# Two rings for the split weights of a two-block mixer kernel: raw units and their low parts share six slots, high parts get five, and loads wait for TensorE

## The reference

```python
def first_block(x, ...):
    for layer in range(DEPTH):
        h = rms_norm(x, norm_mix_pre[layer])
        m = mixer_block(h, ...)                  # h @ w_in, three branches, gates, @ w_out
        x = x + rms_norm(m, norm_mix_post[layer])
        h = rms_norm(x, norm_ffn_pre[layer])
        x = x + rms_norm(swiglu(h, ...), norm_ffn_post[layer])
...
def second_block(x, c, ctx, ...):
    for l in range(DEPTH):                       # the context is updated in layer 0 alone
        hx = rmsnorm(x, norm1_w[l]) * (1.0 + sc1) + sh1
        mix_x, mix_c = token_mixers(hx, hc, ...) # h @ w_in, conv, mLSTM, attention, @ w_out
        x = x + g1 * mix_x
        hx = rmsnorm(x, norm2_w[l]) * (1.0 + sc2) + sh2
        x = x + g2 * conv_ffn(hx, ...)
```

## Time and profile before

| | |
|---|---|
| median of 3 runs | 2644.31 us (2641.03 to 2645.47) |
| the profiled execution | 2644.44 us, of it 2642.3 us span |
| granted TensorE clock | 0.999 on the mean |
| TensorE busy | 2603.2 us (99%) |
| TensorE loading weights | 2243.4 us (85%) |
| VectorE busy | 1487.3 us (56%) |
| ScalarE busy | 1340.1 us (51%) |
| GpSimd busy | 1666.2 us (63%) |
| HBM read | 382.53 MB, 145 GB/s over the span |

### The profile page before, as it was taken

One profiled execution on the slowest core, in us unless ns is written; L12 is line 12 of the kernel. 1 busy time (PEld: TensorE's weight loads), 2 busy tenths in 40 slices (PEclk: granted clock), 3 DMA queues, 4 the chain that ended last, 5 costly groups with the idle time before them and its releaser, 6 DMA issues.

```text
span 2642.3 us, 43046 instructions
## 1 busy us (share of the span) xinstructions
PE 2603.2 (99%) x15736; PEld 2243.4 (85%) x15736; DVE 1487.3 (56%) x2545; ACT 1340.1 (51%) x2671; POOL 1666.2 (63%) x1252
## 2 busy tenths in 40 slices
PE   8999999999999999999999999999999999999999
PEld 7998788899888887877788888888888889999888
DVE  6886533388654436855533333668654965235644
ACT  6475545556655553456343343442444575446655
POOL 6779788778887884422334345556554645558887
PEclk9999999999999999999999999999999999999999
DMA  6466676545867552221222223446542423335555
GB/s 220 133 188 209 209 241 190 167 133 160 255 211 223 182 179 91 88 65 56 65 71 80 72 88 114 133 144 225 204 135 85 142 84 109 105 118 161 169 181 162
DMA packets 216445, 386.24 MB, mean 146 GB/s; under 512 B 21952, under 2 KB 49856, under 8 KB 216256
## 3 DMA queue, kind: packets, MB, share of 16 engines
q1 hardware_dynamic: 216256, 383.66, 45.8%
HBM read 382.53 MB, written 1.05 MB: 145 GB/s over the span
## 4 chain that ended last, share of the span: by engine, by line
PE 44%; issue 33%; POOL 17%; DVE 4%; ACT 1%; DMA 0%; POOLq 0%; SPq 0%; DVEq 0%; ACTq 0%
POOL w_lo L1065 17%; PE bank L1130 12%; PE bank L1134 6%; PE bank L1114 6%; PE bank L1116 6%; PE bank L1115 6%; PE bank L1679 1%; PE bank L1230 1%; PE bank L1210 1%; PE bank L1211 1%; PE bank L1212 1%; PE bank L1652 1%; PE bank L1346 1%; DVE k_dec L2604 0%; DVE gdec L2599 0%
## 5 line engine op out<-in xcount | busy, mean ns | idle before, releaser
L1065 POOL TENSOR_TENSOR w_lo<-raw,w_hi 128x512 fp32r<-128x512 f32 x1248 | 1666.0, 1366 | 965.5 <-ACT w_hi L1733 964.4
L1733 ACT ACTIVATE w_hi<-raw 128x512 fp32r<-128x512 f32 x1248 | 719.0, 623 | 295.5 <-PE bank L1116 125.3
L1114 PE MATMUL bank<-hl,w_hi 128*128 128x256 f32 (+1 forms) x1920 | 659.8, 344 | 0.8 <-POOL w_lo L1065 0.3
L1116 PE MATMUL bank<-hl,w_lo 128*128 128x256 f32 (+1 forms) x1920 | 645.4, 336 | 0.0
L1115 PE MATMUL bank<-hl,w_hi 128*128 128x256 f32 (+1 forms) x1920 | 645.2, 336 | 0.0
L1114 PEld LDWEIGHTS bank<-hl,w_hi 128*128 128x128 f32 x1920 | 364.2, 190 | 44.1 <-issue 5.0
L1115 PEld LDWEIGHTS bank<-hl,w_hi 128*128 128x128 f32 x1920 | 364.4, 190 | 40.6 <-issue 3.6
L1116 PEld LDWEIGHTS bank<-hl,w_lo 128*128 128x128 f32 x1920 | 364.2, 190 | 38.0
L1130 PE MATMUL bank<-hl,w_hi 128*128 128x512 f32 x1296 | 361.4, 395 | 0.8 <-POOL w_lo L1065 0.5
L1130 PEld LDWEIGHTS bank<-hl,w_hi 128*128 128x128 f32 x1296 | 221.5, 188 | 31.8 <-issue 3.0
L1134 PEld LDWEIGHTS bank<-hl,w_lo 128*128 128x128 f32 x1296 | 197.7, 188 | 27.6
(11 more groups left out here) (353 smaller groups left out, 4225.3 us busy)
## 6 DMA issues: line engine op xcount, KB each, us to landing
raw<-stream SPq DMA_DIRECT2D x1248, 256.0 KB, 3.0
mix<-stream SPq DMA_DIRECT2D x64, 512.0 KB, 4.7
spare_lo<-stream SPq DMA_DIRECT2D x16, 512.0 KB, 5.0
spare_hi<-stream SPq DMA_DIRECT2D x16, 512.0 KB, 5.6
xs<-x_rows SPq DMA_DIRECT2D x4, 256.0 KB, 6.0
xs<-ctx_rows SPq DMA_DIRECT2D x1, 1024.0 KB, 6.5
out_rows<-xs SPq DMA_DIRECT2D x8, 128.0 KB, 2.9
dec<-decay SPq DMA_DIRECT2D x1, 768.0 KB, 6.7
```

The lines of the kernel that those rows point to most:

```text
L1065: nc.gpsimd.tensor_tensor(w_lo[:, unit % SPLIT, part], raw[:, unit % RAW, part], w_hi[:, unit % SPLIT, part], ALU.subtract).then_inc(lo_re ...
L1114: nc.tensor.matmul(acc, wh, x[:, 0, k, c0:c1], start=k == 0, stop=False)
L1116: last = nc.tensor.matmul(acc, wl, x[:, 0, k, c0:c1], start=False, stop=k == t.k - 1)
L1733: nc.scalar.activation(w_hi[:, n % SPLIT, part], raw[:, n % RAW, part], ACT.Copy).then_inc(hi_ready, 1)
```

## The change

The 44 KB of weight buffers per partition are cut anew. `raw` gets six slots instead of three. `w_lo` becomes a second name for the same bytes, so POOL writes the low part over the raw weights that it has just read. `w_hi` gets five slots instead of four. A load of unit n can then no longer follow POOL: it waits until TensorE has used unit n-6, once for both halves. ACT's copy of unit n waits for unit n-5 and stands one unit earlier in its program, wherever the place was counted with `SPLIT`. Weight loads have the key n-6 in SP's order. POOL's loop has 30 units in its body.

```diff
-RAW, SPLIT = 3, 4
+RAW, HIGH, FIRST = 6, 5, 3
...
-    order = [(n - RAW - SPLIT, 0, n) for n in range(N_UNITS)]
+    order = [(n - RAW, 0, n) for n in range(N_UNITS)]
...
+    at_raw = sbuf.at
     raw = sbuf.put("raw", [P, RAW, UNIT * P])
-    w_hi = sbuf.put("w_hi", [P, SPLIT, UNIT * P], F32R)
-    w_lo = sbuf.put("w_lo", [P, SPLIT, UNIT * P], F32R)
+    w_lo = nc.alloc_sbuf_tensor_at("w_lo", [P, RAW, UNIT * P], F32R, offset=at_raw)
+    w_hi = sbuf.put("w_hi", [P, HIGH, UNIT * P], F32R)
...
             def load(unit):
+                if unit >= RAW:
+                    kind, count = PLACE.free[unit - RAW]
+                    sp.wait_ge(tile_done if kind == "tile" else unit_used, count)
                 for j, part in enumerate(UNIT_HALVES):
-                    if unit >= RAW:
-                        sp.wait_ge(lo_ready, 2 * (unit - RAW) + j + 1)
                     sp.dma_start(raw[:, unit % RAW, part], stream[ADA_UNITS + unit][:, part])\
                         .then_inc(raw_loaded[unit % RAW][j], 16)
...
-            for unit in range(1, RAW):
+            for unit in range(1, FIRST):
...
-            step = RAW * SPLIT
+            step = RAW * HIGH
...
-                    nc.gpsimd.tensor_tensor(w_lo[:, unit % SPLIT, part], raw[:, unit % RAW, part],
-                                            w_hi[:, unit % SPLIT, part], ALU.subtract).then_inc(lo_ready, 1)
+                    nc.gpsimd.tensor_tensor(w_lo[:, unit % RAW, part], raw[:, unit % RAW, part],
+                                            w_hi[:, unit % HIGH, part], ALU.subtract).then_inc(lo_ready, 1)
...
-                    if n >= SPLIT:
-                        kind, count = PLACE.free[n - SPLIT]
+                    if n >= HIGH:
+                        kind, count = PLACE.free[n - HIGH]
...
-                split_through(first // UNIT + SPLIT - 1 if t.wide == 2 else last + SPLIT - 1)
+                split_through(first // UNIT + HIGH - 1 if t.wide == 2 else last + HIGH - 1)
...
-                split_through(min(at["unit"] + count - 1, at["freed"] + SPLIT))
+                split_through(min(at["unit"] + count - 1, at["freed"] + HIGH))
```

More of the change, by code:

```diff
@@ L1036, in _ @@
             sp.dma_start(cst[:, 2 * P:], consts[:, 2 * P:]).then_inc(cst_loaded, 16)
-            load(RAW)
+            load(FIRST)
             sp.dma_start(gmask[:, :, :], gla_masks.rearrange("p (h n) -> p h n", n=P)).then_inc(tables_loaded, 16)
             sp.dma_start(pos_i[:, :], positions).then_inc(tables_loaded, 16)
-            load(RAW + 1)
+            load(FIRST + 1)
             sp.dma_start(dec[:, :, :], decay.rearrange("p (h n) -> p h n", h=RH)).then_inc(tables_loaded, 16)
-            load(RAW + 2)
+            load(FIRST + 2)
             sp.dma_start(xs[:, :, 0:SEQ], ctx_in).then_inc(ctx_loaded, 16)
@@ L1049, in _ @@
                     load_modulation(n)
-                elif n >= RAW + 3:
+                elif n >= FIRST + 3:
                     load(n)
@@ L1107, in product @@
                         wait_block(b + k)
-                        slot, i = (b + k) // UNIT % SPLIT, (b + k) % UNIT
-                        wh, wl = w_hi[:, slot, i * P:(i + 1) * P], w_lo[:, slot, i * P:(i + 1) * P]
+                        u, i = (b + k) // UNIT, (b + k) % UNIT
+                        wh, wl = w_hi[:, u % HIGH, i * P:(i + 1) * P], w_lo[:, u % RAW, i * P:(i + 1) * P]
                         if late and late[1] == k:
@@ L1128, in high @@
                     def high(k):
-                        w = w_hi[:, (b + k) // UNIT % SPLIT, (b + k) % UNIT * P:((b + k) % UNIT + 1) * P]
+                        w = w_hi[:, (b + k) // UNIT % HIGH, (b + k) % UNIT * P:((b + k) % UNIT + 1) * P]
                         return nc.tensor.matmul(acc[:, :], w, x[:, :, k, c0:c1], start=k == 0, stop=k == t.k - 1)
                     def low(k):
-                        w = w_lo[:, (b + k) // UNIT % SPLIT, (b + k) % UNIT * P:((b + k) % UNIT + 1) * P]
+                        w = w_lo[:, (b + k) // UNIT % RAW, (b + k) % UNIT * P:((b + k) % UNIT + 1) * P]
                         return nc.tensor.matmul(acc[:, 0:SEQ], w, x[:, 0, k, c0:c1], start=False, stop=False)
@@ L1171, in side_by_side @@
                             wait_unit(u)
-                            wh, wl = w_hi[:, u % SPLIT, k * P:(k + 1) * P], w_lo[:, u % SPLIT, k * P:(k + 1) * P]
+                            wh, wl = w_hi[:, u % HIGH, k * P:(k + 1) * P], w_lo[:, u % RAW, k * P:(k + 1) * P]
                             nc.tensor.matmul(acc[:, c0:c1], wh, x[:, 0, k, c0:c1], start=k == 0, stop=False)
@@ L1208, in values @@
                             wait_block(b + 2 * k)
-                            wh, wl = w_hi[:, u % SPLIT, j * P:(j + 2) * P], w_lo[:, u % SPLIT, j * P:(j + 2) * P]
+                            wh, wl = w_hi[:, u % HIGH, j * P:(j + 2) * P], w_lo[:, u % RAW, j * P:(j + 2) * P]
                             nc.tensor.matmul(acc, h_hi[:, k, c:c + P], wh, start=k == 0, stop=False)
@@ L1732, in split_through @@
                         act.wait_ge(raw_loaded[n % RAW][j], 16 * (n // RAW + 1))
-                        nc.scalar.activation(w_hi[:, n % SPLIT, part], raw[:, n % RAW, part], ACT.Copy).then_inc(hi_ready, 1)
+                        nc.scalar.activation(w_hi[:, n % HIGH, part], raw[:, n % RAW, part], ACT.Copy).then_inc(hi_ready, 1)
                     at["unit"] += 1
```

## The result

The changed kernel takes 2651.95 us (median of 7 runs, 2649.76 to 2656.25) against 2643.89 us (median of 7, 2641.03 to 2645.47) for the kernel before. The ratio is 1.0033, 95% interval 1.0024 to 1.0043: 8 us slower. Its profiled execution took 2651.95 us, the span in it is 2650.1 us, 7.8 us longer than before. Lines of the changed kernel have numbers two higher than before (L1067 is the subtraction, L1735 the copy, L1005 the load).

The account below looks back on a forecast made before the run. TensorE was taken to bound the kernel. Span 2642.3 - 2.1 (gains) + 1.2 (start) = 2641.4 us; with 2.1 around it 2643.5, and 2643.4 since the profiled execution was 0.1 above its median; range 2638 to 2650 us.

Parts of the forecast that it names:

- What bounds the kernel: First block's feed-forward: TensorE sets the pace at 2.80 us a unit; POOL, at 2.52, keeps up with 10% to spare.
- The rival that the supply binds: Eight restarts behind a norm would each gain a unit of POOL's time, 20 us: 2624 us; chance 8%.
- The gains, 2.1 us: TensorE's waits for POOL removed: 0.99 us at a down projection, 0.50 and 0.64 in the second block's layer 1.
- Load lead and the even stretch: Loads land well before TensorE needs them; ACT waits some 0.2 us longer a unit, and nothing reaches TensorE.
- The value tiles, 0: Eight `mv` places: ACT's copies come 1.7 us late, covered by 1.87 us of idle; without cover, 14 us.
- SP's queue, "I take 0": Modulation loads one weight load earlier cost 0, since both come to the moment when the same unit is finished.
- ACT stalls on landing data: Rival: ACT's copies wait for late loads and the eight value tiles are not covered, 14 us: 2658 us; chance 10%.
- The start, 1.2 us (0 to 1.8): Empty pipeline: POOL loses its 2.35 us pause at 46.3 us, which slows VectorE; cost 1.2 us, between 0 and 1.8.
- The subtraction in place, 0: POOL's subtraction over its own input moves as many bytes and takes 1.25 us again; no cost.

Follow-up runs that it names:

- e5: Changed kernel with both old orders: weight loads at key n-7 and ACT's copies three units ahead, not four; 2642.45 us, ratio 0.9998.
- e1: Changed kernel with only SyncE's weight-load key back at n-7, so weight loads stand one modulation place earlier again; 2646.25 us, ratio 1.0010.
- e2: Kernel before, old rings and waits, with the changed kernel's load order in SyncE's queue (key n-6); 2644.08 us, ratio 1.0001.
- e4: Changed kernel with ACT's copies back in the old order, three units ahead of the tile taken, not four; 2643.55 us, ratio 1.0000.
- e6: Changed kernel with key n-7, and GpSimd starting unit 9's low part only after VectorE has finished the rotation angles; 2644.64 us, ratio 1.0004.
- e3: Changed kernel with GpSimd starting unit 8's low part only after VectorE's CAST of the positions; 2648.45 us, ratio 1.0021.
- e7: Changed kernel with key n-7 and ACT's copies three units ahead up to unit 14, four after; 2644.99 us, ratio 1.0008.
- e10: Changed kernel with SyncE's key at n-5, so modulation loads stand one more weight load earlier; 2677.38 us, ratio 1.0131.
- e9: Changed kernel with key n-7 and six extra constant matmuls on TensorE ahead of the first `k_dec`; 2646.71 us, ratio 1.0013.
- e11: Changed kernel with both old orders, but ACT's copies four units ahead in units 278 to 299 and 550 to 574; 2643.88 us, ratio 1.0001.
- e8: Kernel before with GpSimd starting unit 9's low part only after VectorE has finished the rotation angles; 2644.53 us, ratio 1.0003.
- e12: Changed kernel with key n-7 and extra constant matmuls in both TensorE waits at the start, for `rq_raw` and `k_dec`; 2645.99 us, ratio 1.0009.

## Why the prediction was wrong

The forecast was 2643.4 us with a range up to 2650; the time is 2651.95. By its own steps, against the forecast span of 2641.4 us (8.7 less than measured):

- *What bounds the kernel.* Right. The even stretch still has 2.80 us a unit: in the timeline of the changed kernel, to be held against the earlier trace rows, TensorE's rows of the same turn start 2.80 us apart and POOL has its 0.55 us of idle:

```profile
847.69 1.32 PE L1132 MATMUL bank<-hl,w_hi 128*128 128x512 f32 x5
...
850.49 1.31 PE L1132 MATMUL bank<-hl,w_hi 128*128 128x512 f32 x5
850.55 2.54 POOL L1067 TENSOR_TENSOR w_lo<-raw,w_hi 128x512 fp32r<-128x512 f32 x2 [0.55 <-ACT w_hi L1735]
```

  The rival that the supply binds, 20 us of gain, is refuted by the changed kernel: its copies go a unit further ahead and it gains 1.8 us by them. (e5 alone would not show it, since its copies are three units ahead as before.)
- *The gains, 2.1 us.* 1.1 us came at the down projection (0.99 forecast), 0.7 at the up projection (0.64). The 0.50 at 2038.29 did not: TensorE gains 0.08 us around there, held by VectorE's `hl` rows in its place. The gain comes with ACT's copies a unit ahead: e5, which has the rings alone, shows none. The wait of 1.72 us at the last `hid` row stayed, and grew to 2.39.
- *Load lead and the even stretch.* Right: ACT's waits for raw data grew from 57.9 us in 71 places to 142.0 in 134, and none of it reached TensorE there.
- *The value tiles, 0.* Right. ACT waits 1.67 us for the data behind the first value tiles of the stretch of the earlier trace rows, as against the 1.7 us forecast, and TensorE loses nothing.
- *SP's queue, "I take 0".* This is the step that failed: 5.2 us, of them 1.6 by the clock that fell behind the wait. I argued that the modulation loads and the weight loads both come to the same unit's end. I did not ask what the modulation loads wait for, which is not TensorE: it is the old contents being read by VectorE (`o_ret`), and that came 3.6 us after unit 199's slot was free (669.91 against 666.34). Once they stand ahead of a weight load, it waits with them. The load then also landed 5.8 us after its issue, where I had reckoned with 3.0. e1 shows that the order is needed for the loss, e2 and e4 that without ACT's earlier copy it costs 0.65 and 1.2 us there.
- *ACT stalls on landing data*, the 10% rival. Its mechanism is the true one, at another place. It was priced at the value tiles, where the cover held, and not at the gates, where a table load and a take stand behind the copy, and TensorE waits for that take.
- *The start, 1.2 us (0 to 1.8).* Right in cause, three times too small: 3.9 us at unit 40. e4 and e5 show that ACT's earlier copy is behind it, e6 that an undisturbed VectorE delivers `k_dec` before TensorE needs it. What the estimate missed is that VectorE's operations do not just lose a share of POOL's former pause: one of them can be shut out for the whole run. That is worth 2.1 us: with the CAST at 0.29 us (e3) 1.8 are left, the upper end of the range. It is not all, since e1 has a CAST of 1.43 us and 2.7 lost. The clock adds 0.3 us here, up to 1.2 in other runs. The forecast had no term for the clock, though it falls once in the trace of before as well, behind the last `hid` row.
- *The subtraction in place, 0.* Right, 1365 ns against 1366.

The terms add up: 5.2 for the queue, 2.7 more at the start, 0.3 of gains missing, 0.5 at the last `hid` rows, make the 8.7 us.

What stays open: what e7's median would be without the spread of single executions, where the 1.6 us of the remainder lie that the traces do not place, what decides whether the clock falls after a wait of 1.7 or 2.9 us, and what decides between a CAST of one subtraction and one of eight.

## What to carry to other kernels

A deeper ring is two changes at once: more slots, and work that moves in the programs of every engine whose order is derived from the ring's depth. Here the slots were free of cost and of use (e5), and the two moved orders cost 9.5 us, some 4.6 of them only together.

For every item that moves ahead in an in-order queue, write down what it waits for and what then stands behind it. A transfer moved ahead of another must not wait for a later event, and a copy moved ahead of a take must have its data by then. Slack hid the step in the kernel before (e2, within 1 us); with the copies a unit earlier it cost 5.7 us, and one place more another 25 (e10).

When an engine's loss at one point is read, follow it further: of 5.1 us at unit 13, 1.2 were given back 27 units on, most of what the clock had cost there, because another engine was waited for in that stretch. Where TensorE itself sets the pace, behind the gate, the clock's 1.6 us came on top of the wait and stayed.

## What the runs showed of the hardware

- A VectorE operation can be shut out by more than one GpSimd instruction. A CAST of 128x256 from int32 to fp32 took 0.29 us alone, 0.66 to 1.43 us when one subtraction was in its way (five runs, with 2.71 in a sixth), 7.65 to 7.70 us in three runs beside six of them and 10.14 to 10.21 us in four runs beside eight, in these seven until GpSimd paused. TENSOR_SCALAR operations beside the same kind of run took 1.27 us each and took turns. The Trainium skill (SBUF — State Buffer, SBUF: two separate sides) says that the pair of ports that the two engines share is an exclusive lock: a GpSimd instruction, or a VectorE one in a two-port mode or with two inputs in SBUF, has it for the whole instruction, whichever starts first. In which mode the CAST ran no trace shows. The 1.27 us agree with it, as one subtraction takes 1.25; it does not say who has it next, and there the CAST lost up to eight times in a row. In e1 the same instruction at the same place in the same unbroken run lost once (1.43 us).
- TensorE's granted clock fell from 1.00 to 0.50 in or just behind a wait of 2.1 us (changed kernel and e9, at the start), of 2.8 us (changed kernel, at the gate) and of 3.1 us (e1), and stayed there for some 3 to 6 us after work had come back. Twice it did not fall after one wait of 2.9 us (e4, e7), and in e11 it did; after 1.7 us at the last `hid` row it fell in the kernel before and e2 and not in e4, e5 and e8. The fall cost 1.6 us in each of two places where TensorE sets the pace. Matmuls on constants in the waits kept it at 1.00 (e12).
- A weight load of 256 KB landed 3.1 us after its issue in the median of 1248, and after 5.8 us behind two loads of 512 KB (changed kernel at 671.18 us, e4 at the same place).
